# A two-kind mixer model on one core: branch products between gate blocks, decay rows in strips, branch sums on VectorE

## The reference, cut to what matters

```python
u = h @ w_in
(fq, fk, fv, ff, gq, ..., z, xbc, dt, gates) = split_cols(u, IN_SPLITS)
y_a = forgetting_attention(...)   # s + c[t] - c[s], c = cumsum(log_sigmoid(f))
y_b, y_c = ...                    # gated linear attention, retention
o_d = ssd_chunked(...)            # decay = exp(cs[t] - cs[s]), cs = cumsum(dt * a), 8 heads
g = jax.nn.sigmoid(gates.reshape(bsz, seq, N_BRANCH, D_MODEL))
merged = (g[:, :, 0] * (y_a @ w_up_a) + g[:, :, 1] * (y_b @ w_up_b)
          + g[:, :, 2] * (y_c @ w_up_c) + g[:, :, 3] * (y_d @ w_up_d))
return merged @ w_out
```

## Time and profile before

| | |
|---|---|
| median of three runs | 2533.28 us |
| profiled execution | 2533.16 us |
| its span | 2531.5 us |
| TensorE busy | 2498.4 us (99%) |
| VectorE busy | 1807.9 us (71%) |
| ScalarE busy | 1518.3 us (60%) |
| GpSimd busy | 152.5 us (6%) |
| granted clock | 0.998 |
| HBM traffic | 250 GB/s over the span |

### The profile page before, as it was taken

One profiled execution on the slowest core, in us unless ns is written; L12 is line 12 of the kernel. 1 busy time (PEld: TensorE's weight loads), 2 busy tenths in 40 slices (PEclk: granted clock), 3 DMA queues, 4 the chain that ended last, 5 costly groups with the idle time before them and its releaser, 6 DMA issues.

```text
span 2531.5 us, 32026 instructions
## 1 busy us (share of the span) xinstructions
PE 2498.4 (99%) x11892; PEld 2059.5 (81%) x11892; DVE 1807.9 (71%) x1807; ACT 1518.3 (60%) x1579; POOL 152.5 (6%) x131
## 2 busy tenths in 40 slices
PE   8999999999999999999999999999999999999998
PEld 7888888888888888878888877888888888888876
DVE  6577655657775554565455567988888989898988
ACT  6554544555554454545445555777777777777776
POOL 0101100010020000020000013000000000000010
PEclk9999999999999999999999999999999999999999
DMA  6444555444455564445554456999999999999996
GB/s 258 150 157 159 183 183 184 175 159 150 152 181 184 189 209 154 176 167 182 189 189 156 163 183 227 381 368 385 375 381 378 378 381 375 382 368 381 367 401 253
DMA packets 90683, 633.76 MB, mean 250 GB/s; under 512 B 10462, under 2 KB 10838, under 8 KB 15841
## 3 DMA queue, kind: packets, MB, share of 16 engines
q1 hardware_dynamic: 85584, 616.63, 65.2%
q0 software_dynamic: 4720, 15.57, 1.7%
q10 hardware_dynamic: 288, 0.33, 0.0%
HBM read 625.00 MB, written 7.48 MB: 250 GB/s over the span
## 4 chain that ended last, share of the span: by engine, by line
PE 94%; issue 2%; ACT 2%; DVE 2%; DMA 1%; DVEq 0%; SPq 0%; ACTq 0%
PE bank L745 13%; PE bank L747 13%; PE bank L746 13%; PE bank L1264 7%; PE bank L1262 7%; PE bank L1263 7%; PE bank L1235 4%; PE bank L1237 4%; PE bank L1236 4%; PE bank L727 4%; PE bank L760 3%; PE bank L762 3%; PE bank L761 3%; ACT w_hi L1352 1%; PE bank L1135 1%
## 5 line engine op out<-in xcount | busy, mean ns | idle before, releaser
L1791 DVE TENSOR_TENSOR w_lo<-raw,w_hi 128x2048 fp32r<-128x2048 f32 x583 | 1342.4, 2303 | 435.0 <-ACT w_hi L1352 423.4
L1352 ACT ACTIVATE w_hi<-raw 128x2048 fp32r<-128x2048 f32 (+1 forms) x588 | 1120.9, 1907 | 266.3 <-PE bank L762 109.2
L745 PE MATMUL bank<-w_hi,xhi 128*128 128x512 f32 x1456 | 579.3, 398 | 0.8 <-DVE w_lo L1801 0.2
L747 PE MATMUL bank<-w_lo,xhi 128*128 128x512 f32 x1456 | 568.2, 390 | 0.0
L746 PE MATMUL bank<-w_hi,xlo 128*128 128x512 f32 x1456 | 567.6, 390 | 0.0
L1262 PE MATMUL bank<-w_hi,xhi 128*128 128x512 f32 x896 | 358.7, 400 | 0.8 <-issue 0.4
L1264 PE MATMUL bank<-w_lo,xhi 128*128 128x512 f32 x896 | 350.0, 391 | 0.0
L1263 PE MATMUL bank<-w_hi,xlo 128*128 128x512 f32 x896 | 349.5, 390 | 0.0
L745 PEld LDWEIGHTS bank<-w_hi,xhi 128*128 128x128 f32 x1456 | 273.7, 188 | 61.7 <-issue 4.1
L747 PEld LDWEIGHTS bank<-w_lo,xhi 128*128 128x128 f32 x1456 | 273.4, 188 | 58.5
L746 PEld LDWEIGHTS bank<-w_hi,xlo 128*128 128x128 f32 x1456 | 274.0, 188 | 53.4
(11 more groups left out here) (369 smaller groups left out, 2430.7 us busy)
## 6 DMA issues: line engine op xcount, KB each, us to landing
raw<-in_wexpert SPq DMA_DIRECT2D x336, 1024.0 KB, 5.2
raw<-in_wdense SPq DMA_DIRECT2D x248, 1024.0 KB, 4.7
expert_rows<-y POOLq DMA_DIRECT2D x7, 512.0 KB, 4.6
expert_rows<-back POOLq DMA_DIRECT2D x3, 512.0 KB, 3.8
x<-in_x SPq DMA_DIRECT2D x2, 512.0 KB, 4.5
raw<-in_wdense SPq DMA_DIRECT2D x4, 256.0 KB, 6.0
biasT<-bias_rows POOLq DMA_DIRECT2D x1, 1024.0 KB, 6.9
normal_rows<-hnorm POOLq DMA_DIRECT2D x1, 1024.0 KB, 9.1
```

Of the source, the lines that this page charges most:

```text
L745: mm(bank[banks[t]][:, :], xhi[:, k0 + k, tok], wh, start=start and k == 0, stop=False)
L747: last = mm(bank[banks[t]][:, :], xhi[:, k0 + k, tok], wl, start=False, stop=stop and k == 3)
L1352: return nc.scalar.activation(dst, src, f, **kw)
L1791: V.tensor_tensor(lo[:, c % RAW, :], raw[:, c % RAW, :], hi[:, c % HI, :].bitcast(F32), ALU.subtract).then_inc(lo_ready, 1)
```

## The change

- Type 2: the branch products are no longer one piece behind the gates. Branch `br` has a chunk of its own (`pair_chunks`, both halves `n`), and stands behind gate step 14, 18, 22 or 24 (`UP_AT`). The `y` are transposed at steps 11, 20 and 23 (`Y_AT`; `y` 1 needs no transposes). The banks of the gemm blocks swap (`gbank`), and the products get other banks (`up_banks`).
- Type 2: the first half of `merged` is transposed in the middle of the last gate step. The first chunk of `w_out` goes by column halves (`by_columns`), so that it can start on banks 0 and 1.
- Both types: the second half of `merged` is transposed in the middle of the second chunk of `w_out` instead of in front of it. In type 1 the first half is transposed one branch later, after (1, 2), into banks 0 and 1.
- Type 1: the decay rows. `zs` holds the 12 columns of `z` spread over 32-partition strips (column s of strip j is head j). One product at step 4 puts all rows into one bank, `crow` keeps them as high and low parts, row 32j + s. Each head's row is then spread over 128 partitions by a matmul over the 32 rows of its strip (`row_over`), with a one in the wanted row of the weights (`strip_one`). Four heads stand in four strips.
- GpSimd adds no branches. VectorE adds branches 1 and 2 inside `shares`.

```diff
@@ the streams, the steps, the banks
+UP_AT = {14: 0, 18: 1, 22: 2, 24: 3}
+Y_AT = {11: 0, 13: 1, 20: 2, 23: 3}
...
-        tri = sb("tri", [P, 384], F32R)
-        zhi = sb("zhi", [P, NT, 12], F32R)
-        zlo = sb("zlo", [P, NT, 12], F32R)
+        tri = sb("tri", [P, 256], F32R)
+        zs = sb("zs", [P, 2, NT, P], F32R, at=eq_at)
+        crow = sb("crow", [P, 2, S], F32R)
+        strip_one = sb("strip_one", [P, 8], F32R)
...
-            return ((0, 1), (2, 3), (0, 1) if n else (X[0], X[1]), (X[2], X[3]))[br]
+            if k[0] == "mix1":
+                return ((0, 1), (2, 3), (X[0], X[1]), (X[2], X[3]))[br]
+            if n == 0:
+                return (0, 1) if br == 3 else (2, 3)
+            return (X[2], X[3]) if br < 2 else (X[0], X[1])
+
+        def mbank(k, i):
+
+            return (0, 1, X[0], X[1])[i] if k[0] == "mix1" else (X[2], X[3], X[0], X[1])[i]
@@ TensorE
+            def row_over(hs, r, parts, final):
+
+                for a in range(2):
+                    for i, (o, n) in enumerate(parts):
+                        for h in hs:
+                            p = slice(32 * (h % 4), 32 * (h % 4) + 32)
+                            last = mm(bank[X[h % 4]][:, o:o + n], strip_one[p, r:r + 1].to_broadcast([32, P]), crow[p, a, 0:n],
+                                      start=(a, i) == (0, 0), stop=a == 1 and final)
+                            if a == 1 and final:
+                                last.then_inc(full[X[h % 4]], 1)
...
+                    for a in range(2):
+                        mm(bank[b][:, 0:S], zs[:, a, 0, :], tri[:, :], start=a == 0, stop=False)
+                        last = mm(bank[b][:, P:S], zs[:, a, 1, :], tri[:, 0:P], start=False, stop=a == 1)
+                    last.then_inc(full[b], 1)
...
                     for h in hs:
-                        b, o = X[h], bank[X[h]]
-                        pe.wait_ge(free[b], use((k, f"fs{h}"), b))
-                        for n, zz in enumerate((zhi, zlo)):
-                            mm(o[:, 0:3 * P], zz[:, 0, h:h + 1].to_broadcast([P, P]), tri[:, :], start=n == 0, stop=False)
-                            mm(o[:, 2 * P:3 * P], zz[:, 1, h:h + 1].to_broadcast([P, P]), tri[:, 0:P], start=False, stop=False)
+                        pe.wait_ge(free[X[h]], use((k, f"fs{h}"), X[h]))
+                    row_over(hs, 0, ((0, P), (P, S)), False)
...
+                    row_over(hs, 1 if pos == 24 else 2, ((0, S),), True)
...
+                    for n in range(2):
+                        banks = up_banks(k, n, br)
+                        for b in banks:
+                            pe.wait_ge(free[b], use((k, "up", n, br), b))
+                        for kk in range(2):
+                            o = (2 * n + kk) * 512
+                            for t in range(NT):
+                                xh, xl = (yrow(k, 2 * br + kk, part)[:, t * P:t * P + P] for part in range(2))
+                                b = bank[banks[t]][:, :]
+                                mm(b, xh, hi[:, h, o:o + 512], start=kk == 0, stop=False)
+                                mm(b, xl, hi[:, h, o:o + 512], start=False, stop=False)
+                                last = mm(b, xh, lo[:, s, o:o + 512], start=False, stop=kk == 1)
+                        last.then_inc(up_done if n == 0 else w_used, 1)
@@ VectorE
+                    if br in (1, 2):
+                        for t in range(NT):
+                            b0, b = up_banks(k, n, 0)[t], up_banks(k, n, br)[t]
+                            if br == 1:
+                                dve.wait_ge(free[b0], ev((k, "up", n, 0), b0))
+                            else:
+                                dve.wait_ge(T[added], at(added, l, (4 if first else 2) * n + t + 1))
+                            dve.wait_ge(free[b], ev((k, "up", n, br), b))
+                            m = u[:, t, n * 512:n * 512 + 512]
+                            V.tensor_tensor(m, m, gates[:, t, br * 1024 + n * 512:br * 1024 + n * 512 + 512], ALU.add).then_inc(T[added], 1)
...
+                    if not first and pos in UP_AT:
+                        br = UP_AT[pos]
+                        conv(c0 + up_step(br) + 2)
+                        dve.wait_ge(up_done, UPS[k, br])
+                        shares(0, br)
+                        if br == 3:
+                            last_sums(0)
+                        else:
+                            dve.wait_ge(w_used, c0 + up_step(br) + 1)
+                            shares(1, br)
+                    if not first and pos == 25:
+                        split_merged(0)
+                        dve.wait_ge(w_used, c0 + up_step(3) + 1)
+                        shares(1, 3)
+                        last_sums(1)
@@ GpSimd
+                G.memset(zs[:, :, :, :].bitcast(F32), 0.0).then_inc(strips_zeroed, 1)
...
-                            G.tensor_tensor(m, m, gates[:, t, br * 1024 + n * 512:br * 1024 + n * 512 + 512], ALU.add).then_inc(T[name], 1)
```

More of the change, by code:

```diff
@@ L176, in block_chunks, with pair_chunks @@
     return out + [downs[J - 1]]
+def pair_chunks(ws):
+    return [w.reshape(2, P, 2, 512).transpose(1, 2, 0, 3).reshape(P, 2048) for w in ws]
 def dense_stream(v):
@@ L1071, in mixer @@
                     n, half = divmod(pos, 2)
-                    banks = [gbank(n, t) for t in range(NT)]
+                    banks = [gbank(n, t, k) for t in range(NT)]
                     if half == 0:
@@ L1075, in mixer @@
                             pe.wait_ge(free[b], use((k, "gemm", n), b))
-                    gemm_half(banks, c0 + pos, 4 * half, half == 0, half == 1, middle=(lambda: rest_of_norm(k)) if pos == 0 else lambda: None)
+                    gemm_half(banks, c0 + pos_step(k, pos), 4 * half, half == 0, half == 1,
+                              middle=(lambda: rest_of_norm(k)) if pos == 0 else (lambda: merged_columns(0)) if not first and pos == 25 else lambda: None)
                     if pos == 0:
@@ L1142, in mixer, with other_columns @@
-                c += ny
-                for b in range(4):
+                    for i in range(1, ny):
+                        if i == 3:
+                            pe.wait_ge(T["y_ssd"], at("y_ssd", l))
+                        turn_y(i, ys[i])
+                    branches()
+                c = c0 + 2 * nb + ny
+                for b in range(4) if first else range(2):
                     pe.wait_ge(free[b], use((k, "out"), b))
+                def other_columns():
+                    for b in (2, 3):
+                        pe.wait_ge(free[b], use((k, "out"), b))
@@ new lines, in last_sums, with split_merged @@
+                def last_sums(n):
+                    dve.wait_ge(T[added], at(added, l, 4 * n + 4 if first else 2 * n + 6))
+                    for t in range(NT):
+                        b = up_banks(k, n, 3)[t]
+                        dve.wait_ge(free[b], ev((k, "up", n, 3), b))
+                        m = u[:, t, n * 512:n * 512 + 512]
+                        V.tensor_tensor(m, m, gates[:, t, 3072 + n * 512:3072 + n * 512 + 512], ALU.add).then_inc(T[name], 1)
+                def split_merged(half):
+                    for i in (2 * half, 2 * half + 1):
+                        b, done = mbank(k, i), "m_hi" if first else "m_hi_b"
+                        dve.wait_ge(T[done], at(done, l, i + 1))
+                        V.scalar_tensor_tensor(out=mlo[:, 2 * i:2 * i + 2, :], in0=bank[b][:, :].rearrange("p (j t) -> p j t", j=2), scalar=0.5,
+                                               in1=mhi[:, 2 * i:2 * i + 2, :].bitcast(F32), op0=ALU.mult, op1=ALU.subtract).then_inc(free[b], 1)
@@ L2229, in mixer @@
                             negative_lambda()
-                    if pos == (30 if first else 22):
+                    if first and pos == 30:
                         split_y(k, 0)
-                for i in range(1, ny):
-                    split_y(k, i)
-                mixb = 8 if first else 5
-                name, added = ("whole", "merged") if first else ("whole_b", "merged_b")
-                def shares(n, br):
-                    out_of(k, mixb + 2 * br + n)
-                    for t in range(NT):
-                        b = up_banks(n, br)[t]
-                        gg = gates[:, t, br * 1024 + n * 512:br * 1024 + n * 512 + 512]
-                        dst = u[:, t, n * 512:n * 512 + 512] if br == 0 else gg
-                        V.scalar_tensor_tensor(out=dst, in0=gg, scalar=1.0, in1=bank[b][:, :], op0=ALU.add, op1=ALU.mult).then_inc(free[b], 1)
@@ L2261, in mixer @@
[L2261 to L2273 removed]
+                    elif not first and pos in Y_AT:
+                        split_y(k, Y_AT[pos])
```

362 lines of the change are left out of this document (195 added, 167 removed).

## The result

The changed kernel takes 2517.52 us, the median of four runs (2516.84 to 2518.38). The kernel before took 2532.73 us beside it (four runs, 2531.78 to 2533.73). The ratio is 0.9938, with a 95% interval from 0.9925 to 0.9950: 15.2 us faster, where the forecast was 2518.1 us. The profiled execution took 2516.84 us, with a span of 2515.2 and a granted clock of 0.998.

What follows compares the result with a forecast made beforehand. The prediction took TensorE, busy 2498.4 of 2531.5 us, to bound the kernel. Its terms 7.9 + 6.6 + 0.6 = 15.1 us, taken from 2533.2, gave 2518.1 us, with a range from 2515.0 to 2525.5.

Steps and rivals of the forecast that it cites:

- Term 1: End of the type-2 mixer: three TensorE waits, 3.9 us a layer, go away; gain 7.9 us over two layers.
- The count of VectorE's queue: End of type 2: merged half ready 6.8 us after branch 3's products start, asked for at 8.2, margin 1.4.
- Term 2: Type-1 decay rows: strip matmuls make steps 6, 7, 24 and 27 cheaper, 3.3 us a layer; gain 6.6 us.
- the step on draining: Type-1 decay rows: draining at a tiling-mode change is already in the traced strips, bounded at tenths of a microsecond.
- rows 6: Trace rows of existing strip matmuls: 24 on 32 rows take 0.89 us, 24 on 64 rows take 1.65.
- Term 3: Sums moved from GpSimd to VectorE, type-1 end: layer 0 gains 0.5, layer 1 loses 0.5; together 0.6 us gained.
- A: Rival on the decay rows: strips do not overlap, gain only 11.2 us, 2522.0 us; chance 0.10.
- B: Rival at the mixer ends: VectorE becomes the bound, the 1.4 us margin fails, gain 6.5, 2526.7 us; chance 0.12.
- C: Rival: delayed weight splits on VectorE make TensorE wait at type-2 gate steps, slower, 2536.5 us; chance 0.04.

Runs made afterwards that it cites:

- e2: The changed kernel with the old type-1 decay rows instead of the strips: 2522.55 us, ratio 0.9958.
- e3: The changed kernel with the additions of branches 1 and 2 back on GpSimd, in both types: 2516.02 us, ratio 0.9932.
- e6: The changed kernel with type 2's first merged half transposed in front of the last gate step instead of in its middle: 2521.7 us, ratio 0.9957.
- e4: The changed kernel with type 1's split of the first merged half ahead of the last two additions on VectorE: 2515.64 us, ratio 0.9931.
- e9: The changed kernel plus eight strip matmuls at type 1's steps 24 and 27, over four strips (layer 0) or one (layer 1): 2520.95 us, one run.
- the third series: The last set of runs, beside the kernel before (2532.16 us, 9 runs); the changed kernel, run again in it, took 2519.05 us, ratio 0.9949.
- e11: The kernel of e7 once more, run beside the changed kernel: 2514.79 us, ratio 0.9932.
- e5: The changed kernel with the rows of all four fox heads made at step 6 and none at step 7: 2517.78 us, ratio 0.9942.
- e7: The changed kernel with the edits of e4 and e5 together: 2514.92 us, ratio 0.9930.
- e8: The changed kernel with the same strip matmuls ordered head by head, successive ones in the same strip: 2519.43 us, ratio 0.9946.
- e1: The kernel before with the new decay rows in strips and nothing else of the change: 2526.6 us, ratio 0.9975.

## Why the prediction was right, point by point

- **Term 1, forecast 7.9, measured 7.86.** The three waits are gone, each type-2 mixer is 3.93 us shorter. e2 has it without the strips and e3 without the additions on VectorE, so the new order is enough for it. The count of VectorE's queue (6.8 us to the merged half, margin 1.4) came out at 6.9 and 1.46, and e6 took that margin away. The count was closer than its own terms: 4.2 + 4 x 0.6 is 6.6, and the trace has 4.4 for the end of the split and 0.62 an operation. e3 adds what the text did not say: the additions on VectorE had no part in this term.
- **Term 2, forecast 6.6, measured 5.5.** From its first transpose of `x` to its first branch product each type-1 mixer is 2.76 us shorter instead of 3.3. Of this, steps 24 and 27 were right (1.77 to 0.43, where 1.76 to 0.40 was said), steps 6 and 7 (0.66 for 0.69) and the product at step 4 (0.48 for 0.44). What failed is the step on draining, "the 0.89 us of rows 6 already contain one such entry". The price of the entry lies before the group, between the last full-height matmul and the first strip: 0.31 instead of 0.23. The gate step in front of a group is 0.09 longer at steps 6, 24 and 27 (at step 6 it is 5.73, where the same step took 5.64 before) and 0.06 longer at step 7, and the matmuls behind the groups of steps 24 and 27 take 0.05 more (11.06 us for 48, before 11.00). That is 0.43 us a layer, 0.9 in all. The rest is the product at step 4, which waits 0.1 for `z` in layer 0, and hundredths. The rule of the Trainium skill (TensorEngine Tiling (Array Packing), Key Properties) that a change of mode drains the array fits this: the change of mode had its price, 0.9 us in sum, far below the gain.
- **Term 3, forecast 0.6, measured 0.4.** From the first branch product to `w_out` the text counted 28.96 us (229.24 to 258.2) with a wait of 0.5 to 0.8. The trace has 226.29 to 255.32, 29.03, with a wait of 0.62. Layer 0 gains and layer 1 loses, as said: to the end of the mixer +0.7 and -0.3. e4 shows that this term could have been 1.9 larger.
- **The rivals.** A is out: e9's one-strip group costs 1.35 where four strips cost 0.66. B did not come, and e6 shows where it begins. C did not come: no gate step of type 2 waits for `w_lo`.
- **The sum.** The terms give 7.86 + 5.5 + 0.4 = 13.8, which is the difference of the mixers, where 15.1 was forecast. The medians gave 15.2 in the first comparison and 2532.16 - 2519.05 = 13.1 in the third series. So part of the closeness of 2517.52 to 2518.1 is chance. The four runs behind 2517.52 all had a granted clock of 0.998; in the third series the one run of the changed kernel with 0.998 took 2517.21 us, and four with 0.997 took 2518.93 to 2519.84. And in the profiles the expert part, in which nothing changed, measures 982.5 to 985.2 us. The traces show two places where it wanders: its first 65 us, by the clock (e11 above, and e5, e7 and e8 with the same 0.92), and a stretch of some 20 us near its end. Waits there, before (2425 to 2448 us) and after (2411 to 2434 us):

```profile
ACT w_hi L1352 <- DMA raw<-in_wexpert: 7.2, 6, 2.2
PE bank L1235 <- DVE glo L2378: 1.8, 2, 1.5
...
ACT w_hi L1450 <- DMA raw<-in_wexpert: 2.9, 4, 1.5
PE bank L1333 <- DVE glo L2518: 0.8, 1, 0.8
```

  ScalarE waits for weights that come late, 7.2 us before and 2.9 after, and the same 76 matmuls take 20.1 us before and 18.2 after (from the 3991st to the 4067th of the part). That is most of the 2.3 us between the two profiled expert parts, and no work of the change. Why the weights are later in some executions, no run shows.

## What to carry to other kernels

Cost a wait at the end of a phase by adding up the whole queue of the engine waited for, from its last free moment: here that count was right to 0.1 us twice (6.8 for 6.9 and 28.96 for 29.03, the first with some luck in its terms), and e6 shows that it also says how much earlier a step may stand. When work moves onto a busy engine, ask which of it the next stage needs first: the same additions cost 0.9 us a layer ahead of the awaited operation and at most 0.3 behind it. Row strips are paid by their busiest strip plus about 0.2 us for the group, 0.06 to 0.09 in front of it and up to 0.05 behind, so fill all four strips in one group and make few groups.

## What was not expected of the hardware

- Strip matmuls overlap in whatever order they are issued (0.44 against 0.43 us for eight), and one of a free strip starts ahead of earlier ones that wait for a busy strip.
- The entry into strips costs 0.06 to 0.09 us, and is seen in the gap before the group, not in it.
- After 2.02 us of standing still the clock fell to its lower level for 3 us, twice in one profiled execution (e1), and did not in another after 2.07, nor after 1.18. Waits of this length have a price of their own, and it varies.
- Where GpSimd adds beside it (e3), VectorE's weight split takes 3.18 us again instead of 2.29, and e3 is no slower for it. Its timeline of VectorE:

```profile
251.04 1.28 DVE L2351 SCALAR_TENSOR_TENSOR mlo<-bank,mhi 128x512 fp32r<-128x512 f32 x2
252.24 3.18 DVE L1899 TENSOR_TENSOR w_lo<-raw,w_hi 128x2048 fp32r<-128x2048 f32 x1
```

  The split of `merged` is through before that. The Trainium skill (SBUF — State Buffer, two separate sides) says that a VectorE operation with two SBUF inputs and a reading GpSimd operation exclude each other. The 0.9 us fit this, if VectorE waits for the rest of an addition that has already begun (a whole one takes 1.94); what it waits for is not seen in the trace.
